# A hybrid decoder step on one core: the adaLN bias added after the turn, small loads put first, and spare products in the opening

## The reference, cut to what matters

```python
def adaln(c, w, b):
    mod = jax.nn.silu(c) @ w + b
    shift, scale, gate = jnp.split(mod, 3, axis=-1)
    return shift[:, None, :], scale[:, None, :], gate[:, None, :]
...
hp = rmsnorm(yp, norm_g[layer]) * (1.0 + sc_p) + sh_p
hs = rmsnorm(ys, norm_g[layer]) * (1.0 + sc_s) + sh_s
...
yp = yp + gt_p * op
ys = ys + gt_s * os_
```

## Time and profile before

| | |
|---|---|
| median of the runs | 698.2 us (three runs, 698.19 to 698.54) |
| the profiled execution | 697.32 us |
| its span, first to last instruction | 695.1 us |
| mean granted clock of TensorE | 0.977 of full |
| TensorE busy with products | 632.0 us |
| VectorE, ScalarE, GpSimd busy | 359.8, 215.3, 197.6 us |
| bytes moved | 190.27 MB, mean 274 GB/s |

### The profile page before, as it was taken

How to read it: one execution, slowest core, us unless ns; L and a number is a source line. 1 busy time by engine, 2 the same in 40 slices (tenths; PEclk the granted TensorE clock), 3 DMA queues, 4 the chain that set the end, 5 groups by cost and what they waited for, 6 DMA issues and landing times. The chain is left out here.

```text
span 695.1 us, 11063 instructions
## 1 busy us (share of the span) xinstructions
PE 632.0 (91%) x4217; PEld 369.5 (53%) x4217; DVE 359.8 (52%) x702; ACT 215.3 (31%) x458; POOL 197.6 (28%) x221
## 2 busy tenths in 40 slices
PE   4889999999999999899999999999899968769986
PEld 1547646665666667344344556777544435434442
DVE  2332856576655758363200633446538478984722
ACT  3345243513442342111010625453324224421010
POOL 0032228043404712220000358999701011110000
PEclk9899999999999999999999999999999989988998
DMA  9995336973885389838996553545699999999980
GB/s 324 362 394 206 122 121 240 347 237 114 314 312 191 122 301 335 326 136 294 339 387 241 206 165 132 190 164 189 227 409 405 401 408 405 405 402 397 349 322 8
DMA packets 82048, 190.27 MB, mean 274 GB/s; under 512 B 4103, under 2 KB 12311, under 8 KB 81868
## 3 DMA queue, kind: packets, MB, share of 16 engines
q1 hardware_dynamic: 80322, 183.60, 71.6%
q0 software_dynamic: 1120, 4.46, 1.8%
q10 hardware_dynamic: 554, 1.51, 0.6%
HBM read 167.14 MB, written 22.41 MB: 273 GB/s over the span
## 5 line engine op out<-in xcount | busy, mean ns | idle before, releaser
L550 POOL TENSOR_TENSOR weights_low<-ring,weights_high 128x512 fp32r<-128x512 f32 x80 | 101.0, 1297 | 51.4 <-PE bank L732 39.5
L743 PE MATMUL bank<-weights_high,h_high 128*128 128x512 f32 x272 | 109.1, 401 | 0.0
L743 PE MATMUL bank<-weights_high,h_low 128*128 128x512 f32 x272 | 106.9, 393 | 0.0
L1224 ACT ACTIVATE weights_high<-ring 128x1024 fp32r<-128x1024 f32 x72 | 74.2, 1054 | 88.0 <-PE bank L751 78.7
L751 PE MATMUL bank<-weights_low,h_high 128*128 128x512 f32 x272 | 82.7, 401 | 0.9 <-DVE weights_low L550 0.9
L1833 DVE STREAM_TRANSPOSE ring<-ring 128x1024 f32<-128x1024 f32 x48 | 55.2, 1209 | 19.2 <-DMA ring<-in_cache_k 19.2
L743 PEld LDWEIGHTS bank<-weights_high,h_high 128*128 128x128 f32 x272 | 51.1, 188 | 26.1 <-issue 14.8
L1670 DVE TENSOR_TENSOR partial_low<-bank,partial_high 128x512 fp32r<-128x512 f32 x26 | 17.9, 688 | 89.7 <-ACT partial_high L1179 48.3
L711 PE MATMUL bank<-ring,arena 128*128 128x512 f32 x128 | 58.6, 595 | 0.0
L751 PEld LDWEIGHTS bank<-weights_low,h_high 128*128 128x128 f32 x272 | 49.8, 188 | 14.4 <-DVE weights_low L550 3.9
L743 PEld LDWEIGHTS bank<-weights_high,h_low 128*128 128x128 f32 x272 | 51.2, 188 | 11.1
(11 more groups left out here) (237 smaller groups left out, 924.4 us busy)
## 6 DMA issues: line engine op xcount, KB each, us to landing
ring<-in_w_ada SPq DMA_DIRECT2D x12, 2048.0 KB, 14.4
ring<-in_cache_k SPq DMA_DIRECT2D x48, 512.0 KB, 11.7
ring<-in_cache_v SPq DMA_DIRECT2D x40, 512.0 KB, 9.0
ring<-in_w_ret_in SPq DMA_DIRECT2D x8, 2048.0 KB, 9.4
ring<-in_state_ret SPq DMA_DIRECT2D x32, 512.0 KB, 8.1
out_state_sample<-ring SPq DMA_DIRECT2D x32, 512.0 KB, 6.3
ring<-in_w_moba_in SPq DMA_DIRECT2D x8, 2048.0 KB, 8.7
arena<-in_cache_v SPq DMA_DIRECT2D x24, 512.0 KB, 9.2
```

Source lines behind the costliest of these rows:

```text
L550: tensor_tensor(w_low[:, slot, k, :], ring[:, slot, k * CH:(k + 1) * CH], high[:, k, :].bitcast(F32), ALU.subtract).then_inc(low_ready[LOW ...
L743: pe.matmul(o[i][:, :], xs[p][i][:, k, :], high[:, k, :], start=k == 0 and p == 0, stop=False)
L1224: nc.scalar.activation(w_high[u[0] == "moba"][:, 2 * i:2 * i + 2, :].rearrange("p a b -> p (a b)"), w[:, 2 * i * CH:(2 * i + 2) * CH], ACT ...
```

## The change

The bias of the four chunks in `ADA_FIRST` is no longer added by a product in front of the chunk: it is turned once, together with the gains, and added by VectorE where it reads the turned result. For the scale that makes two instructions of one. For the gate chunks the product stays, now over all 128 rows of a bias tile that GpSimd has zeroed. The two loads of c and the identity go to SyncE's queue, ahead of the first w_ada chunk; ScalarE issues the rest of the constants, the gains and, after GpSimd's zeroing, the bias. The opening's order on TensorE, ScalarE and VectorE is another, and products of the identity with itself, which nothing reads, stand at five places (16, 4, 8, 8 and 4 of them, `keep_busy`).

```diff
+        bT = small[:, 448:496].rearrange("p (j c) -> p j c", j=4)
...
             first = sum(n for _, n in CONSTS_FIRST)
+            sp.dma_start(c_rows[0:1, :], t["c_prompt"]).then_inc(c_in, 16)
+            sp.dma_start(c_rows[1:1 + NS, :], t["c_sample"]).then_inc(c_in, 16)
+            sp.dma_start(consts[:, 0:P], t["consts"][:, 0:P]).then_inc(ident_in, 16)
...
                 one = 6 * layer + c
-                pe.matmul(o[0:32, :], ident[0:12, one:one + 1].broadcast_to([12, 32]), bias_ada[0:12, :],
-                          start=True, stop=False)
+                turned = c in ADA_FIRST
+                if not turned:
+                    pe.matmul(o[0:32, :], ident[:, one:one + 1].broadcast_to([P, 32]), bias_ada[:, :],
+                              start=True, stop=False)
                 for k in range(KT):
                     g = 32 * (k % 4)
-                    last = pe.matmul(o[g:g + 32, :], cT[:, k, :], w[:, k, :], start=0 < k < 4, stop=k >= 4)
+                    last = pe.matmul(o[g:g + 32, :], cT[:, k, :], w[:, k, :], start=(0 if turned else 1) <= k < 4,
+                                     stop=k >= 4)
...
-            pe.wait_ge(consts_in, 16)
+            pe.wait_ge(ident_in, 16)
...
-            sealed(pe.transpose(open_bank(("gT",))[:, 0:2 * KT], g_rows[0:2 * KT, :], ident[0:2 * KT, 0:2 * KT]), ("gT",))
+            o = open_bank(("gT",))
+            pe.transpose(o[:, 0:2 * KT], g_rows[0:2 * KT, :], ident[0:2 * KT, 0:2 * KT])
+            pe.wait_ge(bias_in, 16)
+            for j in range(4):
+                last = pe.transpose(o[:, 16 * (j + 1):16 * (j + 1) + 12], bias_ada[0:12, j * P:(j + 1) * P],
+                                    ident[0:12, 0:12])
+            sealed(last, ("gT",))
             wait_read(pe, ("cT",))
-            pe.wait_ge(bias_in, 16)
+            def keep_busy(o, n):
+                for _ in range(n):
+                    pe.matmul(o[:, 0:P], ident, ident, start=True, stop=True, skip_group_check=True)
+
+            keep_busy(bank[3], 16)
+            ada_part(0, ADA_FIRST[0])
+            keep_busy(bank[3], 4)
             pe.wait_ge(sums_ready, 1)
-            for i, c in enumerate(ADA_FIRST):
-                ada_part(0, c)
-                part_turned(0, c)
-                if i == 1:
-                    for n in range(2):
-                        x_turned(0, n, 0)
-                        x_turned(0, n, 1)
-                    x_turned(0, 2, 0)
+            part_turned(0, ADA_FIRST[0])
+            keep_busy(bank[3], 8)
+            ada_part(0, ADA_FIRST[1])
+            for n in range(2):
+                x_turned(0, n, 0)
+                if n == 0:
+                    part_turned(0, ADA_FIRST[1])
+            for n in range(2):
+                x_turned(0, n, 1)
+            ada_part(0, ADA_FIRST[2])
+            x_turned(0, 2, 0)
+            part_turned(0, ADA_FIRST[2])
+            wait_read(pe, ("mT", 0, ADA_FIRST[2]))
+            keep_busy(bank[1], 8)
+            ada_part(0, ADA_FIRST[3])
+            keep_busy(bank[1], 4)
+            part_turned(0, ADA_FIRST[3])
             pe.wait_ge(sample_h, 1)
...
-            act.dma_start(c_rows[0:1, :], t["c_prompt"]).then_inc(c_in, 16)
-            act.dma_start(c_rows[1:1 + NS, :], t["c_sample"]).then_inc(c_in, 16)
             first = sum(n for _, n in CONSTS_FIRST)
-            act.dma_start(consts[:, 0:first], t["consts"][:, 0:first]).then_inc(consts_in, 16)
+            act.dma_start(consts[:, P:first], t["consts"][:, P:first]).then_inc(consts_in, 16)
             act.dma_start(g_rows[0:2 * KT, :], t["norm_g"].rearrange("l (k p) -> (l k) p", p=P)).then_inc(norm_in, 16)
+            act.wait_ge(pool_zeroed, 1)
             act.dma_start(bias_ada[0:12, :], t["b_ada"].rearrange("l (c n) -> (l c) n", c=6)).then_inc(bias_in, 16)
...
             copy_part(("ada", 0, ADA_FIRST[0]))
-            copy_part(("ada", 0, ADA_FIRST[1]))
             norm_row(0, 0)
             norm_row(0, 1)
+            copy_part(("ada", 0, ADA_FIRST[1]))
+            norm_row(0, 2)
             h_rounded(0, 0, 0, 0)
-            norm_row(0, 2)
             h_rounded(0, 1, 0, 1)
...
+            nc.gpsimd.memset(bias_ada[:, :], 0.0).then_inc(pool_zeroed, 1)
             nc.gpsimd.memset(X[:, 2, :], 0.0).then_inc(pool_zeroed, 1)
...
+                bias = bT[:, :, 6 * layer + c].unsqueeze(2).broadcast_to([P, 4, 1 + NS])
                 if c // 2 == 1:
                     gain = gT[:, layer, ks].unsqueeze(2).broadcast_to([P, 4, 1 + NS])
-                    ins = nc.vector.scalar_tensor_tensor(ab[:, 0, ks, :], src, 1.0, gain, ALU.add, ALU.mult)
+                    read_out(nc.vector.scalar_tensor_tensor(ab[:, 0, ks, :], src, 1.0, bias, ALU.add, ALU.add),
+                             ("mT", layer, c))
+                    wait_read(dve, ("mT", layer, c))
+                    link(nc.vector.tensor_tensor(ab[:, 0, ks, :], ab[:, 0, ks, :], gain, ALU.mult))
                 else:
-                    ins = nc.vector.tensor_copy(ab[:, 1, ks, :], src)
-                read_out(ins, ("mT", layer, c))
-                wait_read(dve, ("mT", layer, c))
-                dve.sem_inc(ab_ready, 1)
+                    read_out(nc.vector.tensor_tensor(ab[:, 1, ks, :], src, bias, ALU.add), ("mT", layer, c))
+                    wait_read(dve, ("mT", layer, c))
...
+            read_out(nc.vector.tensor_copy(bT, o[:, 16:80].rearrange("p (j c) -> p j c", j=4)[:, :, 0:12]), ("gT",))
...
             modulation_turned(0, ADA_FIRST[0])
-            modulation_turned(0, ADA_FIRST[1])
             row_norm(0, 0)
             row_norm(0, 1)
+            modulation_turned(0, ADA_FIRST[1])
+            row_norm(0, 2)
             h_scaled(0, 0, 0)
-            row_norm(0, 2)
             h_scaled(0, 1, 0)
```

More of the change, by code:

```diff
@@ L474, in build @@
         half_used = sem("half_used")
-        consts_in, x_in, c_in, gn_in, gains_in, pages_in = (
-            sem(n) for n in ("consts_in", "x_in", "c_in", "gn_in", "gains_in", "pages_in"))
+        consts_in, ident_in, x_in, c_in, gn_in, gains_in, pages_in = (
+            sem(n) for n in ("consts_in", "ident_in", "x_in", "c_in", "gn_in", "gains_in", "pages_in"))
         bias_in, tables_in = sem("bias_in"), sem("tables_in")
         sums_ready, part_high_ready = sem("sums_ready"), sem("part_high_ready")
-        norm_in, ab_ready, diag_ready, sample_h = (sem(n) for n in ("norm_in", "ab_ready", "diag_ready", "sample_h"))
+        norm_in, diag_ready, sample_h = (sem(n) for n in ("norm_in", "diag_ready", "sample_h"))
         k_parts, v_parts = sem("k_parts"), sem("v_parts")
@@ L593, in _ @@
                     sp.dma_start(X[:, 0:2, :], t["x_prompt"][0].rearrange("(n p) d -> p n d", p=P)).then_inc(x_in, 16)
-                    sp.wait_ge(pool_zeroed, 1)
+                    sp.wait_ge(pool_zeroed, 2)
                     sp.dma_start(X[0:32, 2, :], xs).then_inc(x_in, 16)
@@ L1152, in _ @@
                 if s == 0:
-                    pe.wait_ge(pool_zeroed, 3)
+                    pe.wait_ge(pool_zeroed, 4)
                 sample_values(s)
@@ L1442, in _ @@
                 if s == 0:
-                    act.wait_ge(pool_zeroed, 3)
+                    act.wait_ge(pool_zeroed, 4)
                     sample_exps(0)
@@ L1534, in _ @@
             pool.wait_ge(qb_ready, 1)
-            pool.wait_ge(pool_zeroed, 2)
+            pool.wait_ge(pool_zeroed, 3)
             qb = L1["qbT"].rearrange("p (g e j) m -> p g e j m", g=4, e=2)
@@ L1561, in _ @@
             nc.gpsimd.memset(L1["PTs"][:, 2, :], 0.0).then_inc(pool_zeroed, 1)
-            pool.wait_ge(pool_zeroed, 3)
+            pool.wait_ge(pool_zeroed, 4)
             gated = 0
@@ L1701, in _ @@
             o = wait_full(dve, ("gT",))
-            read_out(nc.vector.tensor_copy(small[:, 0:2 * KT], o[:, 0:2 * KT]), ("gT",))
+            nc.vector.tensor_copy(small[:, 0:2 * KT], o[:, 0:2 * KT])
+            read_out(nc.vector.tensor_copy(bT, o[:, 16:80].rearrange("p (j c) -> p j c", j=4)[:, :, 0:12]), ("gT",))
             wait_read(dve, ("gT",))
-            dve.wait_ge(consts_in, 16)
+            dve.wait_ge(ident_in, 16)
             modulation_turned(0, ADA_FIRST[0])
-            modulation_turned(0, ADA_FIRST[1])
             row_norm(0, 0)
             row_norm(0, 1)
+            modulation_turned(0, ADA_FIRST[1])
+            row_norm(0, 2)
             h_scaled(0, 0, 0)
-            row_norm(0, 2)
             h_scaled(0, 1, 0)
```

## The result

The changed kernel takes 694.69 us (median of 20 runs, 691.05 to 699.48) against 698.81 us for the kernel before on the same chip (20 runs, 696.67 to 703.17). The ratio is 0.9921, interval [0.9903, 0.9938]: 5.5 us by the ratio, 4.1 us by the medians. The forecast was 1.75 us. The direction is as forecast, the size is not. The profiled execution took 693.63 us, 3.7 less than that of before (697.32).

What follows compares the result with a forecast made beforehand. TensorE is busy 632.0 of 695.1 us, and everything behind the first projection hangs on its start. 3.0 + 1.45 - 1.3 - 1.4 = 1.75 us off the median gives 696.4 us, range 693.4 to 699.2.

Steps and rivals of the forecast that it cites:

- The new order: Opening up to the first projection: at full clock it starts at 39.6 instead of 42.57 us, 3.0 us gained.
- Small loads in front: Opening: three issues ahead of the bulk on SyncE delay x and all chunks by 0.8 us (0.35 to 1.2).
- Layer 1: Layer 1's w_ada chunks and w_ret_out: no bias saving and one low-clock stretch at 356.3 us, -1.4 us (0 to -3.4).
- the bias saving at 0 of 3.9: Layer 1: four removed bias products free 3.9 us of TensorE, but w_ret_out's landing stays at 356.3, so 0 gained.
- 15.3 us from the section's start: Sign in layer 1: w_ret_out's products keep their 15.3 us distance from the section's start at 341.09 us.
- the clock term of the opening: Opening: clock gain at the first projection, +1.45 us, and a low stretch on the turns of x, -1.3 us.
- "+1.45": First projection: spare products keep full clock, so its sample rows take 1.85 for 3.3 us; 0 if not.
- "-1.3": Opening: one low-clock stretch falls on the turns of x after TensorE's wait, costing 1.3 us (0 to -2.7).
- "the same 1.75 off the median": Whole kernel: the gain summed from one profiled execution, 1.75 us, applied to the median, giving 696.4 us.
- a widening of 2 us either way: Late in the kernel, at waits for keys: a moved start can shift one low stretch in or out, 2 us.
- "The spare products hold the clock everywhere": Rival: no low stretch in the opening or layer 1, 4.45 us gained, 693.8 us; chance 0.14.
- The slower case: Rival: low clock at the first projection's start and for two stretches in layer 1, -1.7 us, 699.9 us; chance 0.15.

Runs made afterwards that it cites:

- order_bias_2: Kernel after without spare products and with c and identity loads back on ScalarE (new order and turned bias stay), second timing: 0.9969, 698.18 us; first timing 0.9986.
- before_4: The kernel before, unchanged, profiled a fourth time: 698.36 us.
- before_3: The kernel before, unchanged, profiled a third time: 704.68 us.
- xwait: Kernel after plus twenty more spare products between the second chunk and the first turn of x: 0.9969 against the kernel before, 698.30 us.
- order_only: Kernel before with only the new order on TensorE, ScalarE and VectorE; bias by product, loads on ScalarE, no spare products: 0.9913, again 0.9914.
- order_bias0: Kernel after without spare products, small loads on ScalarE, bias turned in layer 0 only (a product again in layer 1): 0.9943, 695.38 us.
- no_spare: Kernel after without any of its 40 spare products, all else as changed: 0.9971 against the kernel before, taken again 0.9996.
- after_2: The kernel after, unchanged, profiled a second time: 692.88 us.
- early_spare: Kernel after with nine spare products in the wait for x, none of the eight before the last chunk, layer 1's bias as product: 0.9879, 690.63 us.
- spare_on_before: Kernel before with the 40 spare products alone at their five places; order, bias and loads as before: 1.0064, 703.54 us.

## Why the prediction was right in direction and wrong in size

**The new order: right as a path.** Forecast 3.0 us off the first projection's start at full clock; the profiled pair has 41.22 for the forecast 40.9 (39.6 plus 1.3). The 3.0 us are not the order alone: 1.9 of them are the bias products of the last two chunks, and 1.8 are taken off for spare products. The two timings of the order alone, with neither, give as much as the whole change.

**Small loads in front: nearly right, and neutral.** The delay of x is 0.6 us in the mean of the profiles, for 0.8 taken. The prediction had worked out 1.2 us, the whole issue time, by the rule of the Trainium skill ("DMA: Bandwidth & Descriptors", section "Issuing engines are not separate DMA queues"); the traces show half of that. That the early identity makes room for the sixteen spare products was missed.

**Layer 1: right.** Forecast -1.4 us net with the bias saving at 0 of 3.9; measured -1.1 us for the section (three executions against four; about -0.5 in the profiled pair), by the low stretch on L710. One detail was off: L710 did not begin 15.3 us from the section's start but at 14.24. The 15.3 was a matter of the one execution: the other three of the kernel before have 14.33 to 14.78 us, two of them without any wait for w_ret_out, and the three of the kernel after 14.24 to 14.36. So 0.4 of the 3.9 us came, in the mean. What the Trainium skill ("TensorE: Matmul & The Clock Gate", "HAM oscillation — how this bites in real kernels") says of waits that make the next tile start at half speed is what L710 shows (3.53 us behind a wait of 2.50), and at twice the length order_bias_2 (7 us at 0.51 behind a wait of 3.89).

**The step that failed is the clock term of the opening**, "+1.45" for the first projection and "-1.3" on the turns of x, together 0.15 us, and with it the sentence that took "the same 1.75 off the median". Both fit the profiled execution of before: order and clock were to bring the first high product forward by 3.15 us, and between the two profiled executions it came forward by 2.8. But that execution of before was one of its shorter ones (697.32 us, where the medians of the five sets of runs timed since are 698.8 to 700.8). In two of the other three more of the opening went at half speed: the first high product stands at 47.00 us in before_4 and at 51.99 in before_3, and in the old order the losses in front of x stood on the path, since x waited behind the second chunk. In all fifteen profiles with the new order it stands at 40.77 to 44.47 us. The change is worth 5.3 us there over the profiles, not 3.15.

The experiments show the same step from the side of the spare products. In the sum they bring 1.45 us on the first projection for the 1.8 us of the eight that stand on the path, together -0.35 us. Measured, the kernel without them is 3.5 and 5.2 us slower than the kernel after (0.9971 and 0.9996 against 0.9921). By the profiles 1.8 us of that lie in the opening and 2.3 in layer 1's section, 300 us later, for which the forecast had no term. That the clock carries the first part is read from the profiles and was not made by an experiment of its own; for the second part it is not shown (see what stays open).

The rest of the difference to the forecast is the 1.3 us behind layer 1's section. The forecast named low stretches there as a widening of 2 us either way and gave them no value; the four profiles of the kernel before differ by 1.4 us there among themselves.

**The rivals.** "The spare products hold the clock everywhere" gave 693.8 us, near the 694.69 measured, but that is luck, and not what happened in the profiled execution: the low stretches on x (4.55 us) and on L710 (3.53 us) are there. The slower case came close in kernels without spare products: two low stretches in layer 1 stood in all four profiles with the bias turned in both layers and no spare product, and in xwait, and in all five most of the gain was gone. The turned bias is not the only way to them: the profile of order_only has them too (section 57.3 us), though its timed runs kept the gain.

**What stays open.** Why the bias turned in layer 0 costs something without spare products (0.9943 against 0.9914; the intervals overlap) is argued from the clock alone. The first high product of order_bias0 stands at 42.96 us, with L733 (the first projection's sample rows) at half speed, and the order alone has 43.62 and 41.78. Why the section of layer 1 takes 57.0 to 57.6 us in no_spare, order_bias and xwait, and 55.1 us in the kernel after, 300 us behind the opening, no run tells, since the code there is the same. What the traces add is where it begins, with the transfer of w_ret_out's first chunk. From its issue to its landing, where the trace gives it, it takes 13.2 to 13.6 us in the profiles with a section of 57 us (no_spare, order_bias, order_bias_2, xwait and order_only), and 11.2 to 12.8 us in ten profiles with 53.3 to 55.4 us. In the first four of these, as in after_2, SyncE issues it 2.0 us into the section. TensorE waits 3.5 to 3.9 us for it in these four instead of 2.5, and the low stretch behind that wait is longer. Why the transfer is late was not asked of any experiment, so the clock is not shown to be the first cause there. Whether early_spare beats the kernel after is open too (0.9879 [0.9833, 0.9925] against 0.9921 [0.9903, 0.9938]), and with it what the nine products are worth: it changes three things at once.

## What to carry to other kernels

Before a term for the clock goes into a sum, look at several executions of the kernel: which stretches run at half speed differs between them, and the mean gain of an edit is what it does to all of them. An order that takes work off a chain also takes off that work's worst case. Removing products from a stretch that waits for transfers can cost as much as it saves. Spare products have to be sized to the wait that they fill: twenty in 2.4 us ran over it by 1.9 us, and sixteen ahead of a chunk that everything waited on made the kernel slower. A test that takes a part away from the change and one that puts it alone on the kernel before can disagree, as here for the spare products and the bias; then the parts depend on each other, and only combinations tell.

## What had not been expected of the hardware

The granted clock read 1.00 from 18.5 to 24.2 us in before_3 while a chunk took 3.64 us for 16 records, the duration at half speed (3.64 us at 0.51 in order_bias_2, 1.92 at 1.00). The row had not changed yet in that trace: so early, the durations tell the clock and the row does not. In spare_on_before, too, 32 records of spare products took 5.81 us from 9.89 us on, at a row of 1.00, where 16 records took 2.03 later.

Executions of one unchanged kernel spread over 10 us (693.15 to 703.77 us in 28 runs on one chip), with the stretches at half clock in different places; four profiles of the kernel before had the first high product anywhere from 45.75 to 51.99 us.
